# First layer norm: squares summed over the feature tiles by TensorE's accumulation instead of by VectorE's additions

## The chip, the cores and the metric

The kernel runs on one core of one Trainium2 chip. The metric is the device time of one execution in microseconds (us), the median of several runs. The engines named below are TensorE (PE in the rows; its weight loads are PEld), VectorE (DVE), ScalarE (ACT), GpSimd (POOL) and SyncE (SP), which issues most loads.

## The reference, cut to what matters

The program is one inference step of a hybrid decoder layer on 1024 prompt tokens and 32 sample tokens, 1056 in all, with 1024 features each, in float32. Its two branches (latent attention and a state-space scan) are merged and projected, and then two layer norms stand around a feed-forward network:

```
h = layer_norm(ALPHA * x + mix, ln1_g, ln1_b)
y = layer_norm(ALPHA * h + swiglu_ffn(h, ...), ln2_g, ln2_b)

def layer_norm(x, g, b, eps=1e-5):
    mu  = mean(x, axis=-1)
    var = mean(square(x - mu), axis=-1)
    return (x - mu) * rsqrt(var + eps) * g + b
```

The change concerns `var` of the first norm, that is, of `h`.

## The kernel before, in words

**Layout.** Activations are held with the features on the 128 partitions: `mm` is 128 x 8 x 1056, that is, KT = 8 feature tiles by all tokens. A sum over the features is therefore a sum over 8 tiles and over 128 partitions. The tokens are cut in three thirds of CH = 352 tokens, and a third in four blocks of TS = 88.

**The products.** Each float32 product with weights is written as three products of rounded halves (high by high, high by low, low by high: `whi`, `wlo`, `ahi`, `alo`). One output tile of one third is then 24 matrix products of 352 columns. `dense` makes a whole output tile (72 products), `unit_third(u, c)` that of one third c (24 products). GpSimd splits each weight tile into `whi` and `wlo` (`split`, L780 and L782) when TensorE has finished with the two tiles before.

**The stage in question.** There is no planner. Each engine has an order that is written out by hand, and engines wait for one another with semaphores. Around the first norm TensorE's order (L1594 to L1614) puts the last two output tiles of the projection (6 and 7) and the first two of the feed-forward (0 and 1) third by third, with the norm's small products between them: tiles 6 and 7 of third 0, tile 6 of third 1, `mean(0)`, tile 7 of third 1, tile 6 of third 2, `mean(1)`, `square_sums(0)`, tile 7 of third 2, `spread(0)`, `mean(2)`, `square_sums(1)`, feed-forward tile 0 of third 0, `spread(1)`, tile 1 of third 0, `square_sums(2)`, tile 0 of third 1, `spread(2)`, and the remaining three.

For a third c the norm goes as follows.

- VectorE adds the last two residual tiles and the running sum `srow` (`last_residual`, L2729 and L2734).
- TensorE multiplies `srow` by a matrix of ones (`mean`, L1576), ScalarE copies the result to `murow` (L2042), and VectorE subtracts it from all eight tiles (`centre`, L2741).
- ScalarE squares the eight tiles into `sqb` (128 x 8 x 352, `squares`, two activations, L2049; the traces call this memory `yz`). Before it writes `sqb` again it waits until the products of the third before are done (`sums_done`), and in its order `root_of(c)` of that third stands ahead of the next `squares`.
- VectorE adds the eight tiles to one in three halving steps (`add_squares`, L2748), and counts `squares_added`.
- TensorE sums tile 0 over the partitions: in `square_sums` (L1583) each of the four blocks of 88 tokens is loaded as weights and multiplied by one column of ones, so that one number for each token lands in a column of bank 7. A float32 product like this is two weight loads and two matrix products in the trace: four blocks are `x8`.
- ScalarE takes the root (`root_of`, L2054), VectorE the reciprocal (`inverse`, L2753), TensorE spreads it over the partitions (`spread`, L1591), and ScalarE copies it to `rsrow` (`factor_row`, L2059).
- VectorE scales the eight tiles (L2756), ScalarE adds the bias and rounds to `ahi` (L2064), and VectorE makes `alo` (L2767), all in `split_third`. The feed-forward products of this third wait tile by tile for `alo` (`g_split`).

VectorE's order is `last_residual(0)`, `centre(0)`, `last_residual(1)`, `add_squares()`, `centre(1)`, `inverse(0)`, `last_residual(2)`, `add_squares()`, `split_third(0)`, `centre(2)`, `inverse(1)`, `add_squares()`, `split_third(1)`, `inverse(2)`, `split_third(2)`. The sum of squares of the second norm and of the group norm is made elsewhere and is not touched.

Of the kernel before, what the change touches and what calls it, by code (L numbers as in the profile page):

```python
# [11 lines left out]
ALU = mybir.AluOpType  # L12
# [7 lines left out]
CH = TOK // 3  # L20
# [10 lines left out]
KT = D_MODEL // P  # L31
# [66 lines left out]
TS = 88  # L98
# [49 lines left out]
def build(nc, a, o, stop=99, debug=None):  # L148
# [23 lines left out]
    def sem(name):  # L172
        if name in taken:
            return sem(taken[name][0])
        if name not in sems:
            sems[name] = nc.alloc_semaphore(name)
        return sems[name]
# [52 lines left out]
    def const(name):  # L230
        at, n = where[name]
        return cst[:, at:at + n]

    ident, ones = const("ident"), const("ones")
    V_GATE, V_QN, V_KVN, V_SSM, V_L1G, V_L1B, V_L2G, V_L2B, V_END = 0, 16, 19, 21, 37, 45, 53, 61, 69

    ps = nc.alloc_psum_tensor("ps", [P, 8, 512], F32)
# [160 lines left out]
    mrow, nrow, nshift, nmax, total, ri_ = (ar(n, [P, 1]) for n in ("mrow", "nrow", "nshift", "nmax", "total", "ri_"))  # L398
# [58 lines left out]
    sqb = yz[:, :, :].rearrange("p a n -> p (a n)")[:, 0:KT * CH].rearrange("p (e n) -> p e n", n=CH)  # L457
# [310 lines left out]
    def _(pool):  # L768
# [71 lines left out]
        def ssm_scale(g, c):  # L840
            _, b, l, n = step_of(g, c)
            pool.wait_ge(sem("xd_ready"), k["xd_ready"].next())
            pool.tensor_tensor(s_xe[b][0:n], s_xd[b][0:n], dte[0:n, c, g * HG:(g + 1) * HG].unsqueeze(2).broadcast_to([n, HG, SP_]),
                               ALU.mult).then_inc(sem("xe_ready"), k["xe_ready"].adds(1))
# [64 lines left out]
    def _(pe):  # L909
        k = Counts()  # L910
# [178 lines left out]
        for v in range(2):  # L1089
            for j in range(NCONV // 2):  # L1090
                n = CW + 1 + NB * (CW - 1)
                last = pe.transpose(ps[:, 6 + v, j * n:(j + 1) * n], st[:, (v * 12 + j) * P:(v * 12 + j + 1) * P],
                                    ident[0:n, 0:n])
# [9 lines left out]
        for i in range(9):  # L1103
            n = P if i < 8 else NS
            last = pe.transpose(ps[0:n, 6, i * SH:(i + 1) * SH], dtr[:, i * P:i * P + n], ident[0:SH, 0:SH])
# [7 lines left out]
        last = pe.matmul(ps[0:NS, 6, 256:288], const("same_s")[0:NS], da[0:NS, 8], start=True, stop=True)  # L1113
# [3 lines left out]
        for i in range(8):  # L1117
            last = pe.matmul(ps[0:SH, 7 - i // 4, i % 4 * P:(i % 4 + 1) * P], da[:, i, :], const("causal"), start=True, stop=True)
# [3 lines left out]
        last = pe.matmul(ps[0:SH, 7, 0:NS], da[0:NS, 8, :], const("causal_s")[0:NS], start=True, stop=True)  # L1122
# [4 lines left out]
        for j in range(DI // P):  # L1127
            last = pe.matmul(ps[:, 6, j * NS:(j + 1) * NS], spread[0:SH, j * P:(j + 1) * P], act_[:, SEQ:TOK],
                             start=True, stop=True)
# [9 lines left out]
        def third():  # L1139

            t = thirds_done[0]
            u, c = divmod(t, 3)
            b, free = bank_of(t)
            thirds_done[0] += 1
            if c == 0:
                pe.wait_ge(sem("unit_split"), k["unit_split"].next())
            if t >= LEAD - 1:
                pe.wait_ge(sem(free), k[free].next())
            elif t == 0:
                pe.wait_ge(sem("out_free0"), k["out_free0"].next())  # L1150
            for i in range(3 * KT):
                j, part = divmod(i, 3)
                w, x = ((whi, xhi), (whi, xlo), (wlo, xhi))[part]
                last = pe.matmul(ps[:, b, 0:CH], w[u % SPLIT][:, j * P:(j + 1) * P], x[:, j, c * CH:(c + 1) * CH],  # L1154
                                 start=i == 0, stop=i == 3 * KT - 1)
            done = "unit_done" if c == 2 else "third_done"
            last.then_inc(sem(done), k[done].adds(1))
# [222 lines left out]
        for j in range(2):  # L1380
            for h in range(HEADS):
                last = pe.matmul(ps[:, j, h * NS:(h + 1) * NS], ukt[:, h, j * P:(j + 1) * P], qs[:, h, :], start=True, stop=True)
# [99 lines left out]
        for q in range(NB):  # L1482
            for j in range(2):
                last = pe.matmul(ps[:, 2 + j, q * HT:(q + 1) * HT], oseq[:, q, j * P:(j + 1) * P], const("fold")[:, 0:HT], start=True, stop=True)
        last.then_inc(sem("end_turned"), k["end_turned"].adds(1))
        pe.wait_ge(sem("end_read"), k["end_read"].next(2))
        for h in range(HEADS):
            r = 64 * (h % 2)
            for j in range(2):
                last = pe.matmul(ps[r:r + 64, 7, h // 2 * NS:(h // 2 + 1) * NS], wkv[:, j, h * P + NOPE:(h + 1) * P], olat[:, j, h, :],  # L1490
                                 start=j == 0, stop=j == 1)
# [66 lines left out]
        def unit_third(u, c, ready=None):  # L1558

            s = u % SPLIT  # L1560
            if c == 0:
                pe.wait_ge(sem("unit_split"), k["unit_split"].next())
                pe.wait_ge(sem(f"res_free{s}"), k[f"res_free{s}"].next())
            for i in range(3 * KT):
                j, part = divmod(i, 3)
                if ready and part == 0:
                    pe.wait_ge(sem(ready), k[ready].next())
                w, x = ((whi, ahi), (whi, alo), (wlo, ahi))[part]
                last = pe.matmul(ps[:, 3 * s + c, 0:CH], w[s][:, j * P:(j + 1) * P], x[:, j, third(c)], start=i == 0, stop=i == 3 * KT - 1)
            last.then_inc(sem("unit_done" if c == 2 else "third_ok"), k["unit_done" if c == 2 else "third_ok"].adds(1))  # L1570
# [7 lines left out]
        def square_sums(c):  # L1578

            pe.wait_ge(sem("row_read"), k["row_read"].held())  # L1580
            pe.wait_ge(sem("squares_added"), k["squares_added"].next())
            for t in range(CH // TS):
                last = pe.matmul(ps[0:TS, 7, CH + t:CH + t + 1], sqb[:, 0, t * TS:(t + 1) * TS], ones[:, 0:1], start=True, stop=True)  # L1583
            last.then_inc(sem("sums_done"), k["sums_done"].adds(1))

        def spread(c):
# [4 lines left out]
                last = pe.matmul(ps[:, 7, t * TS:(t + 1) * TS], inv[0:TS, at:at + 1].broadcast_to([TS, P]), ident[0:TS, 0:TS], start=True, stop=True)  # L1591
            last.then_inc(sem("row_ready"), k["row_ready"].adds(1))

        unit_third(6, 0)  # L1594
        unit_third(7, 0)
        unit_third(6, 1)
# [2 lines left out]
        unit_third(6, 2)  # L1599
        mean(1)  # L1600
        square_sums(0)
        unit_third(7, 2)
        spread(0)
# [504 lines left out]
    def _(dve):  # L2108
        k = Counts()
# [12 lines left out]
        step = k["dve_step"]  # L2122
# [26 lines left out]
        def add_squares(to, last):  # L2149
            name = "sq_ready" if last else "dve_step"  # L2150
            dve.tensor_tensor(sq[:, to], sq[:, to], sq[:, 1 - to], ALU.add).then_inc(sem(name), k[name].adds(1))
            if not last:
                dve.wait_ge(step.sem, step.same())
# [568 lines left out]
        def last_residual(c):  # L2722

            for b in range(2):
                if c == 0:
                    dve.wait_ge(sem(f"gt_full{b}"), k[f"gt_full{b}"].next(16))
                dve.wait_ge(sem("unit_done" if c == 2 else "third_ok"), k["unit_done" if c == 2 else "third_ok"].next())
                done = k[f"res_free{b}"] if c == 2 else step
                dve.scalar_tensor_tensor(out=mm[:, 6 + b, third(c)], in0=gt[b][:, third(c)], scalar=ALPHA,  # L2729
                                         in1=ps[:, 3 * b + c, 0:CH], op0=ALU.mult, op1=ALU.add).then_inc(done.sem, done.adds(1))  # L2730
                dve.wait_ge(done.sem, done.same())
                dve.wait_ge(step.sem, step.same())
                total = k["srow_ready"] if b else step
                dve.tensor_tensor(srow[:, third(c)], srow[:, third(c)], mm[:, 6 + b, third(c)], ALU.add).then_inc(total.sem, total.adds(1))  # L2734

        def centre(c):
            dve.wait_ge(sem("mu_ready"), k["mu_ready"].next())
            dve.wait_ge(sem("srow_ready"), k["srow_ready"].same())
            for h in range(2):
                part = mm[:, 4 * h:4 * h + 4, third(c)]  # L2740
                dve.tensor_tensor(part, part, murow[:, third(c)].unsqueeze(1).broadcast_to([P, 4, CH]), ALU.subtract).then_inc(sem("centred"), k["centred"].adds(1))  # L2741

        def add_squares():

            for h in (4, 2, 1):
                dve.wait_ge(sem("squared") if h == 4 else step.sem, k["squared"].next(2) if h == 4 else step.same())
                total = k["squares_added"] if h == 1 else step
                dve.tensor_tensor(sqb[:, 0:h, :], sqb[:, 0:h, :], sqb[:, h:2 * h, :], ALU.add).then_inc(total.sem, total.adds(1))  # L2748

        def inverse(c):  # L2750
            n = CH // TS
            dve.wait_ge(sem("rooted"), k["rooted"].next())
            dve.reciprocal(inv[0:TS, c * n:(c + 1) * n], stat[0:TS, c * n:(c + 1) * n]).then_inc(sem("inverted"), k["inverted"].adds(1))  # L2753
# [16 lines left out]
        last_residual(0)  # L2770
        centre(0)
        last_residual(1)
        add_squares()
        centre(1)
        inverse(0)
        last_residual(2)
        add_squares()
        for b in range(2):
            dve.nop().then_inc(sem(f"gt_free{b}"), k[f"gt_free{b}"].adds(1))
        split_third(0)  # L2780
        centre(2)
        inverse(1)
        add_squares()
        split_third(1)
        inverse(2)
        split_third(2)
# [90 lines left out]
```

## Time and profile before

| | us |
|---|---|
| median of 3 runs | 2907.76 (2906.79 to 2908.07) |
| the profiled execution, its own time | 2900.22 |
| its span, first to last instruction | 2898.4 |
| TensorE busy | 2824.4 (97%) |
| VectorE busy | 1478.2 (51%) |
| ScalarE busy | 736.7 (25%) |
| GpSimd busy | 1015.7 (35%) |
| mean granted clock of TensorE over the span | 0.98 of full |

The profile is of one execution. Its times count from the first instruction. The stage of the first norm lies between about 2048.7 us (tile 6 of third 0) and 2128.5 us (the first ordinary feed-forward tile), under 3% of the span. After it come some 720 us of feed-forward, nearly all of them TensorE products back to back.

### The profile page before, as it was taken

The page shows a single profiled execution, that of the slowest core. Times are in us where ns is not written, and L with a number is a line of the kernel's source. Part 1 is how long each engine was busy: PE and PEld are TensorE (multiplying, and loading weights), DVE is VectorE, ACT ScalarE, POOL GpSimd, SP SyncE. Part 2 cuts the span into 40 slices and gives each one's busy share as a digit, 9 for nine tenths or more (in the row PEclk, how much of TensorE's full clock was granted, in tenths as well). Part 3 has the DMA queues.
Part 4 walks back from the last instruction along what each step waited for, and adds up shares of the span by engine and source line. Part 5 has one row for each costly group of instructions (what it writes and reads, how often), then busy time and mean ns, then how long its engine had stood idle before and what let it go on. Part 6 is the DMA issues. An engine that isn't in the chain of part 4 may idle for free.

```text
span 2898.4 us, 45631 instructions
## 1 busy us (share of the span) xinstructions
PE 2824.4 (97%) x18894; PEld 2532.0 (87%) x18894; DVE 1478.2 (51%) x2052; ACT 736.7 (25%) x1154; POOL 1015.7 (35%) x603
## 2 busy tenths in 40 slices
PE   8999999999999999999999899999899999999998
PEld 7999999899999985555666699999799999999998
DVE  3535787765666665555444448765652222222226
ACT  2111212353545444454423222010220000000000
POOL 3443333333333323444211124344233333333331
PEclk9999999999999998999999999999899999999999
DMA  4263223564656545222343424353211111111111
GB/s 144 72 199 113 81 89 117 172 182 141 178 155 170 159 119 147 65 61 73 142 173 153 156 91 141 117 180 106 65 37 44 44 46 48 43 43 43 51 51 60
DMA packets 314769, 309.72 MB, mean 107 GB/s; under 512 B 32101, under 2 KB 273002, under 8 KB 312138
## 3 DMA queue, kind: packets, MB, share of 16 engines
q1 hardware_dynamic: 252392, 196.02, 23.8%
q10 hardware_dynamic: 58650, 73.89, 7.5%
q0 software_dynamic: 3584, 37.75, 3.4%
q8 instruction: 108, 1.77, 0.3%
q14 instruction: 35, 0.29, 0.0%
HBM read 229.41 MB, written 78.20 MB: 106 GB/s over the span
## 4 chain that ended last, share of the span: by engine, by line
PE 80%; DVE 12%; ACT 3%; issue 3%; DMA 1%; POOL 1%; ACTq 0%; SPq 0%; DVEq 0%; POOLq 0%
PE ps L973 42%; PE ps L1154 12%; PE ps L1288 4%; DVE cv L2252 3%; PE ps L1312 3%; PE ps L1302 2%; PE ps L1446 2%; PE ps L1402 2%; PE ps L1422 1%; PE ps L1187 1%; PE ps L1191 1%; PE ps L1180 1%; DVE cv L2246 1%; DVE cv L2254 1%; PE ps L937 1%
## 5 line engine op out<-in xcount | busy, mean ns | idle before, releaser
L780 POOL TENSOR_TENSOR whi<-raw,cst 128x1024 fp32r<-128x1024 f32 x160 | 311.9, 1949 | 1144.6 <-PE ps L973 937.4
L782 POOL TENSOR_TENSOR wlo<-raw,whi 128x1024 fp32r<-128x1024 f32 x160 | 433.1, 2707 | 12.6
L973 PE MATMUL ps<-ahi,whi 128*128 128x352 f32 x1728 | 375.7, 325 | 2.1 <-POOL wlo L782 1.4
L973 PE MATMUL ps<-alo,whi 128*128 128x352 f32 x1728 | 375.8, 326 | 0.0
L973 PE MATMUL ps<-ahi,wlo 128*128 128x352 f32 x1728 | 372.2, 324 | 0.0
L973 PEld LDWEIGHTS ps<-ahi,whi 128*128 128x128 f32 x1728 | 294.7, 189 | 2.7 <-POOL wlo L782 1.7
L973 PEld LDWEIGHTS ps<-ahi,wlo 128*128 128x128 f32 x1728 | 296.8, 189 | 0.0
L973 PEld LDWEIGHTS ps<-alo,whi 128*128 128x128 f32 x1728 | 295.6, 188 | 0.0
L1154 PE MATMUL ps<-xhi,whi 128*128 128x352 f32 x768 | 255.9, 333 | 0.4 <-ACT xraw L1764 0.4
L1154 PE MATMUL ps<-xhi,wlo 128*128 128x352 f32 x768 | 247.8, 323 | 0.0
L1154 PE MATMUL ps<-xlo,whi 128*128 128x352 f32 x768 | 247.7, 323 | 0.0
L886 POOL TENSOR_TENSOR pr<-pr,rowinv 128x384 f32<-128x384 f32 (+7 forms) x128 | 145.6, 1146 | 191.0 <-DVE rowinv L2458 190.7
L2453 DVE TENSOR_REDUCE negmax<-ps 128x1 f32<-128x384 f32 (+7 forms) x128 | 97.0, 758 | 139.1 <-PE ps L1290 138.4
L1288 PE MATMUL ps<-kb,qb 96*128 96x512 f32 (+3 forms) x384 | 160.2, 535 | 6.5 <-ACT pr L1892 3.3
L2640 DVE TENSOR_TENSOR mm<-ps,mm 128x1056 f32<-128x1056 f32 x80 | 100.6, 1258 | 116.3 <-PE ps L973 116.3
L973 PE MATMUL ps<-xhi,whi 128*128 128x352 f32 x672 | 148.0, 329 | 5.2 <-ACT xraw L1764 3.9
L1288 PEld LDWEIGHTS ps<-kb,qb 96*128 96x128 f32 x384 | 65.0, 196 | 100.4 <-issue 83.1
L1154 PEld LDWEIGHTS ps<-xhi,whi 128*128 128x128 f32 x768 | 144.3, 188 | 8.6 <-issue 6.2
L973 PE MATMUL ps<-xlo,whi 128*128 128x352 f32 x672 | 147.8, 329 | 0.0
L973 PE MATMUL ps<-xhi,wlo 128*128 128x352 f32 x672 | 146.2, 326 | 0.0
L1154 PEld LDWEIGHTS ps<-xlo,whi 128*128 128x128 f32 x768 | 144.4, 188 | 0.0
L1154 PEld LDWEIGHTS ps<-xhi,wlo 128*128 128x128 f32 x768 | 144.3, 188 | 0.0
(368 smaller groups left out, 5031.9 us busy)
## 6 DMA issues: line engine op xcount, KB each, us to landing
raw<-in_w_in SPq DMA_DIRECT2D x61, 512.0 KB, 5.0
s_a<-d_acum SPq DMA_DIRECT2D x32, 512.0 KB, 7.3
d_xbc<-so ACTq DMA_DIRECT2D x24, 528.0 KB, 2.7
gt<-d_g SPq DMA_DIRECT2D x24, 528.0 KB, 3.6
raw<-in_w_ffn_gate SPq DMA_DIRECT2D x22, 512.0 KB, 3.8
raw<-in_w_ffn_up SPq DMA_DIRECT2D x22, 512.0 KB, 3.8
raw<-in_w_ffn_down SPq DMA_DIRECT2D x22, 512.0 KB, 3.5
d_z<-zo ACTq DMA_DIRECT2D x16, 528.0 KB, 5.1
```

The source lines that it names most:

```text
L780: pool.tensor_tensor(whi[s][:, :], raw[:, u], ones[:, 0:1].broadcast_to([P, UNIT]), ALU.mult).then_inc(sem("unit_hi"), k["unit_hi"].adds(1))
L782: pool.tensor_tensor(wlo[s][:, :], raw[:, u], whi[s][:, :].bitcast(F32), ALU.subtract).then_inc(sem("unit_split"), k["unit_split"].adds(1))
L886: pool.tensor_tensor(pr[G][i][:, :], pr[G][i][:, :], rowinv[:, n:n + 1].broadcast_to([P, length]), ALU.mult).then_inc(sem("n_ready"), k["n ...
L973: last = pe.matmul(ps[0:m, 3 * b + c, 0:width], w(j), x[:, j, at:at + width], start=i == 0, stop=i == n - 1)
L1154: last = pe.matmul(ps[:, b, 0:CH], w[u % SPLIT][:, j * P:(j + 1) * P], x[:, j, c * CH:(c + 1) * CH], start=i == 0, stop=i == 3 * KT - 1)
L1288: pe.matmul(ps[:, first_bank + c // 512, 0:w], qb[pp][h][:, q * P:(q + 1) * P], kb[pp][h][:, c:c + w], start=True, stop=True)
L1302: last = pe.transpose(ps[:, 4 + h, c * P:(c + 1) * P], pr[G][2 * (3 - c) + h][:, kb_ * P:(kb_ + 1) * P], ident)
L1312: last = pe.matmul(ps[64 * h:64 * h + 64, 6 + G, c0 * P:512], vb[pp][h][:, kb_, :], ptb[kb_ % 2][h][:, c0 * P:512], start=first, stop=kb_ ...
L1402: last = pe.transpose(ps[:, 4 + i % 3, r * P:(r + 1) * P], src, ident)
L2252: dve.scalar_tensor_tensor(out=cv[b][:, 0:SEQ], in0=xraw[b][:, j:j + SEQ], scalar=tap(j), in1=cv[b][:, 0:SEQ], op0=ALU.mult, op1=ALU.add). ...
L2453: dve.tensor_reduce(negmax[:, n:n + 1], src, AX, ALU.max, negate=True).then_inc(sem("m_ready"), k["m_ready"].adds(1))
L2640: dve.tensor_tensor(thirds(mm[:, e]), out3(b), thirds(mm[:, e]), ALU.add).then_inc(sem(f"res_free{b}"), k[f"res_free{b}"].adds(1))
```

## The change

`square_sums` now multiplies all eight tiles of `sqb`, each block of 88 tokens accumulating over the eight tiles in its column of PSUM: 32 products for a third in place of 4. It waits for ScalarE's two `squared` counts in place of VectorE's `squares_added`. `add_squares` and its three calls go from VectorE's order. Nothing else is moved: the orders of all engines are the same otherwise. The line `k["squared"].n += 16` only sets where TensorE's count of that semaphore begins.

```diff
         def square_sums(c):
 
             pe.wait_ge(sem("row_read"), k["row_read"].held())
-            pe.wait_ge(sem("squares_added"), k["squares_added"].next())
+            pe.wait_ge(sem("squared"), k["squared"].next(2))
             for t in range(CH // TS):
-                last = pe.matmul(ps[0:TS, 7, CH + t:CH + t + 1], sqb[:, 0, t * TS:(t + 1) * TS], ones[:, 0:1], start=True, stop=True)
+                for e in range(KT):
+                    last = pe.matmul(ps[0:TS, 7, CH + t:CH + t + 1], sqb[:, e, t * TS:(t + 1) * TS], ones[:, 0:1], start=e == 0, stop=e == KT - 1)
             last.then_inc(sem("sums_done"), k["sums_done"].adds(1))
...
+        k["squared"].n += 16
         unit_third(6, 0)
...
-        def add_squares():
-
-            for h in (4, 2, 1):
-                dve.wait_ge(sem("squared") if h == 4 else step.sem, k["squared"].next(2) if h == 4 else step.same())
-                total = k["squares_added"] if h == 1 else step
-                dve.tensor_tensor(sqb[:, 0:h, :], sqb[:, 0:h, :], sqb[:, h:2 * h, :], ALU.add).then_inc(total.sem, total.adds(1))
-
...
         last_residual(0)
         centre(0)
         last_residual(1)
-        add_squares()
         centre(1)
         inverse(0)
         last_residual(2)
-        add_squares()
         for b in range(2):
             dve.nop().then_inc(sem(f"gt_free{b}"), k[f"gt_free{b}"].adds(1))
         split_third(0)
         centre(2)
         inverse(1)
-        add_squares()
         split_third(1)
```

## Rows read from the trace of the kernel before

**Rows 1.** The page: span, and each engine's busy time, share and instructions.
```profile
span 2898.4 us, 45631 instructions
PE 2824.4 (97%) x18894; PEld 2532.0 (87%) x18894; DVE 1478.2 (51%) x2052; ACT 736.7 (25%) x1154; POOL 1015.7 (35%) x603
```
**Rows 2.** Stretches: length, busy us of each engine (instructions), granted clock, DMA share, GB/s.
```profile
2071.20:2089.00 17.80, 9.29 (x50) 8.55 (x50) 17.33 (x15) 5.50 (x8) 8.64 (x4) 0.77 0.20 59
2089.00:2104.50 15.50, 12.92 (x45) 11.16 (x46) 13.75 (x22) 7.57 (x12) 0.00 (x0) 0.61 0.00 1
2104.50:2123.50 19.00, 17.72 (x103) 15.17 (x103) 16.36 (x33) 10.67 (x19) 0.07 (x1) 1.00 0.00 0
```
**Rows 3.** Chain that ended last, norm stage: start us, length us, engine, tile, line.
```profile
2054.33 7.97 PE ps L1569 x48
...
2071.21 2.11 DVE yz L2748
...
2073.45 0.85 PE ps L1583 x8
2074.31 5.43 PE ps L1569 x24
...
2082.08 3.69 DVE yz L2748
...
2087.16 0.59 DVE mm L2756
...
2113.45 0.48 ACT rsrow L2059
```
**Rows 4.** Timeline, TensorE: start, length, line, operation, count [idle before, releaser].
```profile
2070.42 0.75 PE L1576 MATMUL ps<-srow,cst 128*128 128x352 f32 x2
2074.61 0.49 PE L1569 MATMUL ps<-alo,whi 128*128 128x352 f32 x1
2074.90 0.49 PE L1569 MATMUL ps<-ahi,wlo 128*128 128x352 f32 x1
...
2087.39 1.31 PE L1583 MATMUL ps<-cst,yz 128*88 128x1 f32 x8 [4.40 <-DVE yz L2748]
...
2098.89 2.01 PE L1591 MATMUL ps<-cst,inv 88*128 88x88 f32 x8 [2.40 <-DVE inv L2753]
...
2106.39 0.71 PE L1583 MATMUL ps<-cst,yz 128*88 128x1 f32 x8
2106.97 0.41 PE L1569 MATMUL ps<-ahi,whi 128*128 128x352 f32 x1
```
**Rows 5.** Timeline, VectorE, the same columns.
```profile
2068.63 4.68 DVE L2748 TENSOR_TENSOR yz<-yz 128x1408 f32<-128x1408 f32 x3
...
2080.32 1.76 DVE L2734 TENSOR_TENSOR srow<-srow,mm 128x352 f32<-128x352 f32 x1
2082.00 5.25 DVE L2748 TENSOR_TENSOR yz<-yz 128x1408 f32<-128x1408 f32 x3
...
2100.19 3.11 DVE L2748 TENSOR_TENSOR yz<-yz 128x1408 f32<-128x1408 f32 x3 [1.36 <-ACT yz L2049]
2103.22 1.08 DVE L2756 SCALAR_TENSOR_TENSOR mm<-mm,vecs,rsrow 128x352 f32<-128x352 f32 x2
```
**Rows 6.** Timeline, ScalarE, the second half of third 0's squares.
```profile
2066.62 1.38 ACT L2049 ACTIVATE yz<-mm 128x1408 f32<-128x1408 f32 x1 [0.15 <-DVE mm L2741]
```
**Rows 7.** Stretches around one-column products and granted clock (columns as in rows 2).
```profile
94.50:96.60 2.10, 2.04 (x25) 1.89 (x25) 0.16 (x1) 0.00 (x0) 2.02 (x4) 1.00 0.00 0
...
97.50:99.40 1.90, 1.90 (x9) 1.90 (x8) 0.00 (x0) 0.00 (x0) 0.00 (x0) 0.54 0.35 96
...
2073.45:2074.20 0.75, 0.75 (x9) 0.75 (x9) 0.75 (x1) 0.00 (x0) 0.75 (x1) 0.84 0.00 0
2074.20:2077.00 2.80, 2.80 (x11) 2.80 (x12) 2.80 (x2) 0.26 (x1) 1.33 (x1) 0.50 0.02 6
2077.00:2079.50 2.50, 2.50 (x16) 2.50 (x15) 2.46 (x5) 2.31 (x2) 0.00 (x0) 0.92 0.69 203
```
**Rows 8.** Timeline, TensorE, group norm (L1506: the same one-column products, 12 blocks).
```profile
1669.59 3.68 PE L1506 MATMUL ps<-cst,sq 128*88 128x1 f32 x24
1673.13 1.23 PE L973 MATMUL ps<-ahi,whi 128*128 128x352 f32 x3
```
**Rows 9.** Stretch with these products (columns as in rows 2).
```profile
1669.60:1673.30 3.70, 3.70 (x27) 3.70 (x26) 2.81 (x3) 3.59 (x4) 0.00 (x0) 0.50 0.00 0
```

## The prediction, made before the changed kernel was timed

> **What bounds the kernel now.** I read the page first: TensorE is busy for 2824.4 of 2898.4 us, VectorE for half of it [rows 1]. So over the whole span TensorE sets the time, and work taken from VectorE is worth something only where TensorE waits for it. That is read from the stage of the first norm alone, in stretches [rows 2]. From 2071.2 to 2089.0 TensorE is busy for 9.3 of 17.8 us and VectorE for 17.3; from 2089.0 to 2104.5 TensorE is busy for 12.9 of 15.5, but at a granted clock of 0.61; from 2104.5 on both are busy at full clock. Here VectorE is the bound and TensorE pays twice, in waits and in a low clock after them. The chain of waits says the same [rows 3]: it runs over the last addition of squares at 2071.21, the one-column products at 2073.45, tile 7 of third 2, the additions at 2082.08, and later VectorE's scaling and low parts. The timelines give the waits: the mean's products end at about 2071.2 and the one-column products of third 0 start at 2073.45, 2.3 us later [rows 3, 4]; those of third 1 start after an idle 4.40 us, ended by the additions [rows 4]; those of third 2 at 2106.39 wait for nothing [rows 4], since the additions were over at 2103.3 [rows 5].
>
> **What goes.** VectorE loses 4.68 + 5.25 + 3.11 = 13.0 us [rows 5], and TensorE its waits of 2.3 and 4.4 us. The squares of third 0 end at 2066.62 + 1.38 = 2068.0 [rows 6], before TensorE's `mean(1)` is done, so its new wait costs nothing there.
>
> **What comes.** Each third has 32 float32 one-column products in place of 4, in the trace's count 64 pairs of weight load and product in place of 8. A pair takes (2106.97 - 2106.39) / 8 = 0.073 us at full clock [rows 4] and (1673.13 - 1669.59) / 24 = 0.147 us at half clock [rows 8, 9]. 64 pairs are 4.7 us at the one and 9.4 us at the other; over three thirds the 168 added pairs are 12.3 to 24.7 us of TensorE time, more than the 6.7 us of waits that go, even at the best clock. That they accumulate in one column I cost at nothing: the two pairs of one float32 product add to one column already.
>
> **Which clock.** In the stretch 94.5 to 96.6 TensorE ran 24 such pairs without a wait to speak of, busy for 2.04 of 2.10 us, and the clock was near half right behind them, 0.54 [rows 7]. From 1669.6 to 1673.3 it was busy all the time, nearly all of it in 24 such pairs, and stayed at 0.50 [rows 9]. After the 2.3 us of idle and 8 pairs from 2073.45 it fell (0.84, then 0.50), and came back within 2077.0 to 2079.5, after some 11 dense products at 0.29 us each in place of 0.166 [rows 3, 4, 7]. So a run of 64 pairs does not hold the clock as dense products do, and the dense unit behind it pays too: 5.43 us for 24 products where full clock needs 3.9 (7.97 / 2) and half clock 7.0 [rows 3, 4]. I take the clock to fall 2.8 us after dense work ends, as at 2071.2 to 2074.0: 38 pairs at 0.073 and 26 at 0.147 are 6.6 us. Where dense work stands right in front, as in third 2, I take 6.0; behind the wait for the last residual, as in third 1, 8.2.
>
> The Trainium skill (TensorE: Matmul & The Clock Gate, "What's actually happening") says that activity releases the throttle and that the clock follows how busy the engine has been. Taken by the busy share, back-to-back pairs would hold the clock at full and even close the waits that make it fall now. By that reading the time comes out as in the second case below, by my reading of rows 7 and 9 as here; the trace speaks against the busy share as the measure, for the engine was busy at 0.97 and 1.00 in those stretches.
>
> **The sum, along TensorE's order.** `square_sums(0)` starts at 2071.2 and takes 6.6: 2077.8, where it ended at 2074.3. Tile 7 of third 2 takes 5.4 as before: 2083.2, against 2079.7. VectorE's last residual and its addition take 2.3 us as before (the addition 1.76, held up beside GpSimd's split, which moves with it) [rows 5]: 2085.5. `mean(2)` 0.7: 2086.2. `square_sums(1)` 8.2: 2094.4, where it ended at 2088.7. ScalarE's squares of third 1 now wait for the root of third 0, at 2078.2, and need 3 us: done by 2081.3, hidden. Meanwhile VectorE starts `split_third(0)` at 2085.5 in place of 2087.16 [rows 3], and has nearly all eight tiles ready at 2094.4. Feed-forward tile 0 runs unhindered, 5.4: 2099.8. VectorE's `centre(2)` and `inverse(1)` are done by then. `spread(1)` and its copy take 1.5: 2101.3, which is where the copy ended before. `split_third(1)` then starts at 2101.3, 1.9 us ahead of 2103.22 [rows 5], because the third addition is gone. That gain is not used, since TensorE is late now: tile 1 of third 0 ends at 2104.4, `square_sums(2)` takes 6.0: 2110.4; tile 0 of third 1, partly at half clock, 5.8: 2116.2; `spread(2)` and the copy 1.5: 2117.7. Before, that copy ended at 2113.45 + 0.48 = 2113.93 [rows 3]. All that follows, the third split that paces the products and 720 us of dense work, is shifted as it is: 3.8 us later.
>
> Where the clock falls within a run varies from one execution to the next. If it falls early, the unit behind stands at 7.0 in place of 5.4. I add 0.7 us for that: +4.5 us. The profiled execution would go from 2900.2 to 2904.7 and its span from 2898.4 to about 2902.9. The median of the runs lies 7.5 us above the profiled one, outside anything this stage does, so I add the 4.5 to it: 2907.8 + 4.5 = 2912.3 us, 0.15% more.
>
> **The cases.**
>
> 1. As above, the pairs at mixed clock: +2 to +8 us, 2912.3. For it: rows 7 and 9. Chance 0.64. A measurement of this kernel can tell about 0.2%, 5.8 us, from no change; a fifth of this case lies above that.
>
> 2. The other side: the clock holds, since TensorE no longer idles in this stage. Then 4.7 us a run and 3.9 a unit: 2071.2 + 4.7 + 3.9 = 2079.8, last residual 2082.1, mean 2082.8, second run 2087.5, tile 0 paced by VectorE's split, which begins at about 2082.3 and ends at 2091.2, `centre(2)` 3.2, inverse, spread and copy 1.8: 2096.2 in place of 2101.4. Then 2095.9 + 3.9 + 4.7 + 3.9 = 2108.4, spread and copy: 2109.4, that is, 4.5 us earlier: 2903.3. It decides from the point at which the clock stays at full through `square_sums(1)` and `(2)`. Against it is the fall at 97.5. Chance 0.11.
>
> 3. The pairs run at half clock throughout or cost 0.1 us or more each even at full clock, and the units behind them stand at 7.0. Against 6.6, 8.2 and 6.0 a run of 9.4 adds 7.4 us, and up to 3 us come from the units, against slack of 0 to 2 us in the split: +8 to +14, 2918.8 in the middle. For it: the clock was at 0.61 from 2089.0 to 2104.5 already [rows 2], so little is needed to keep it down. Chance 0.2.
>
> The remaining 0.05 is for what I don't see, 0.03 of it on the faster side beyond 0.2%. The range is 2905.5 to 2918.5: it leaves out most of case 2 and half of case 3. Slower by over 0.2%: a fifth of case 1 and all of case 3, 0.33. Within 0.2%: the rest of case 1 and nearly all of case 2, 0.62. Faster 0.05: that 0.03, and 0.02 of case 2, whose 4.5 us are not far from 5.8.
>
> **What would show it.** In the changed profile the one-column products come as x64 three times; the first starts at about 2071.2 with no wait, and the second waits for the last residual's mean and not for squares. Each run takes 5.5 to 9 us, and the granted clock falls to half inside it or within 2 us behind. VectorE's busy time is down by 11 to 13 us, TensorE's up by 14 to 22. The copy to `rsrow` of third 2 ends near 2117.7; near 2109 would be case 2, past 2122 case 3. I am wrong if a run takes 4.7 us with dense units of 3.9 behind it, or if the pairs stretch beyond 0.147 us.

## The result, and the profile after

The changed kernel takes 2916.28 us (median of 8 runs) against 2909.48 for the kernel before (8 runs, the three shown above among them). The ratio is 1.0031, with a 95% interval of 1.0021 to 1.0041: 0.31% slower, about 9 us (the two medians differ by 6.8 us). One of the eight runs of the kernel before took 3933.37 us and is left out of the ratio. The forecast was 0.15%, with 2905.5 to 2918.5 as its range. The direction and the range held. The size is twice the forecast, and about half of it has a cause that the prediction did not name.

The page and the chain of waits of the changed kernel (start us, length us, engine, tile, line; x64 are the one-column products):

```profile
span 2911.9 us, 45958 instructions
PE 2839.5 (98%) x19062; PEld 2546.3 (87%) x19062; DVE 1471.5 (51%) x2043; ACT 736.7 (25%) x1154; POOL 1012.2 (35%) x603
```
```profile
2059.17 7.96 PE ps L1569 x48
...
2076.01 6.42 PE ps L1584 x64
2082.42 5.63 PE ps L1569 x24
...
2091.31 7.85 PE ps L1584 x64
2099.16 5.77 PE ps L1569 x24
2104.92 0.86 PE ps L1592 x8
2105.78 3.88 PE ps L1569 x24
2109.67 6.00 PE ps L1584 x64
2115.67 6.02 PE ps L1569 x24
...
2122.58 0.47 ACT rsrow L2061
...
2137.68 163.00 PE ps L973 x1008
2300.68 1.07 issue
2301.75 139.76 PE ps L973 x864
2441.51 0.67 issue
2442.18 139.75 PE ps L973 x864
2581.93 1.08 issue
2583.01 139.78 PE ps L973 x864
2722.80 0.62 issue
```

Set beside [rows 3], the chain has changed hands: where it ran through VectorE's additions, it now stays on TensorE from 2059.17 to 2122.56 but for the last residual of third 2. The first piece shown starts 4.84 us later than in the kernel before (2059.17 against 2054.33). That much comes from the part of the program ahead of the stage, which is the same in both: over the seven profiled executions without instructions added at the start of the program, the stage's first product comes anywhere from 2048.7 to 2058.8 us. So only lengths are compared below, not times.

The stretches name the two terms. First the kernel before, stage and feed-forward, then the changed one (columns as in rows 2):

```profile
2048.70:2128.50 79.80, 64.44 (x344) 58.02 (x342) 65.60 (x84) 27.85 (x41) 19.32 (x9) 0.87 0.11 34
2128.50:2849.50 721.00, 720.95 (x4464) 720.95 (x4465) 182.12 (x128) 47.34 (x44) 266.60 (x124) 1.00 0.15 45
```
```profile
2053.60:2137.70 84.10, 78.72 (x512) 75.83 (x511) 56.12 (x75) 27.71 (x41) 20.11 (x9) 0.86 0.11 32
2137.70:2863.00 725.30, 721.86 (x4464) 720.71 (x4465) 182.13 (x128) 47.34 (x44) 266.96 (x124) 1.00 0.15 46
```

The norm's stage grew from 79.8 to 84.1 us, 4.3 more. The feed-forward, in which nothing is changed, grew from 721.0 to 725.3, another 4.3. Its products are the same 4464, and the loss stands in the chain above: a gap of 0.6 to 1.1 us, put down to "issue", at each of the four places where TensorE's loop jumps back, 3.4 us in all; the chain does not resolve the rest. In the kernel before, this whole stretch has no gap:

```profile
2128.55 720.48 PE ps L973 x4460
```

The queue that carries instructions shows what goes on there (kind, packets, MB, share), first before, then after:

```profile
q8 instruction: 8, 0.13, 0.1%
```
```profile
q8 instruction: 44, 0.72, 0.4%
```

4.3 + 4.3 = 8.6 us are 0.30%, close to the measured 0.31%. These are two single executions, and the stage varies from one to the next (below), so that the sum agrees to 0.01% is partly luck.

### The profile page after: what moved, and what is told of

Its sections match the earlier page's. It is cut to its first block, busy times and chain, and to the rows that moved or that the text cites. A ratio compares the mean times of both kernels' runs of the same rounds, so it can differ in the third digit from the quotient of the medians.

```text
span 2911.9 us, 45958 instructions
## 1 busy us (share of the span) xinstructions
PE 2839.5 (98%) x19062; PEld 2546.3 (87%) x19062; DVE 1471.5 (51%) x2043; ACT 736.7 (25%) x1154; POOL 1012.2 (35%) x603
## 4 chain that ended last, share of the span: by engine, by line
PE 81%; DVE 11%; ACT 3%; issue 2%; DMA 1%; POOL 1%; ACTq 0%; SPq 0%; DVEq 0%; POOLq 0%
PE ps L973 42%; PE ps L1154 12%; PE ps L1288 4%; DVE cv L2254 3%; PE ps L1312 2%; PE ps L1302 2%; PE ps L1422 2%; PE ps L1446 2%; PE ps L1402 2%; PE ps L1569 1%; DVE cv L2248 1%; PE ps L1187 1%; PE ps L1191 1%; PE ps L1180 1%; PE ps L1067 1%
```

## The experiments

Ten kernels were run. All stretches below run from the stage's first product to the first ordinary feed-forward tile ("stage"), and from there to the first product of the last tiles ("feed-forward"). Each ratio is against the kernel before on the same chip. Every kernel was profiled once, so the length of a stage is that of one execution.

**Two theories of the second term.** The program of TensorE has 336 more instructions in front of the loop: 84 products, each in four instructions (two weight loads and two matrix products). Counted in the assembled program, the loop is 1764 instructions long, at 64 bytes 6.9 fetches of 16 KB (0.72 MB in 44). It begins 236 instructions behind a multiple of 256 in the kernel before and 60 behind one in the changed kernel.

The first experiment moves the loop alone, by 80 instructions:

```diff
 (kernel before, start of TensorE's program)
+        for _ in range(160):
+            pe.wait_ge(sem('eps_ready'), 1)
```
(Two such waits on a count that stands already make one instruction.)

> The kernel before, with 80 instructions added at the very start of TensorE's program (each waits for two semaphore counts that stand already), where TensorE idles until 8.5 us for its input. All work is the same; the loop of the feed-forward stands 80 instructions later in the program, which is where the changed kernel has it but for whole multiples of 256 (it has 336 more). Theory A (the 4.4 us that the changed kernel loses after the norm come from fetching TensorE's instructions again at each turn of the loop, because of where the loop stands): the norm stage stays as before, gaps of 0.6 to 1.1 us stand at each of the four jumps back, instruction fetches there go from 8 to about 44, and the kernel is 3 to 5 us slower (0.10 to 0.17%). Theory B (the loss comes from the norm stage, a clock or a buffer that is late): no gaps, 8 fetches, and the same time within 1.5 us.

Measured: ratio 1.0014 (1.0003 to 1.0025), 4.1 us; the medians differ by 2.5. The stage is 81.2 us, the feed-forward 725.1, the fetches are 44, and the gaps are there:

```profile
2142.92 163.04 PE ps L975 x1008
2305.96 1.07 issue
2307.04 139.75 PE ps L975 x864
2446.78 0.78 issue
...
2587.34 0.63 issue
...
2727.72 0.65 issue
```

Theory A holds: with all work as before, the feed-forward is 4.1 us longer, and only the place of the loop differs there. (The padding is not quite free: the first product comes at 9.71 us in place of 8.47, so up to 1.2 us of the timed difference may be the padding's.) The second moves the changed kernel's loop by 176 further, to a whole 512 (`range(352)` at the same place).

> The changed kernel, with 176 such waiting instructions at the start of TensorE's program, so that with the 336 of the products the loop of the feed-forward is moved by 512 in all, twice 256. Theory A: the gaps at the jumps back are gone, the norm stage keeps its loss of 3.5 to 5 us against before, and the kernel is 4 to 5 us slower than before in place of some 9 (0.14 to 0.17%). Theory B: still gaps, still about 0.3% slower.

Measured: 8 fetches, no gap, the feed-forward 720.9, the stage 82.6. But the ratio is 1.0064 (1.0050 to 1.0079). The mechanism is as theory A said; the expected time was missed, because the padding is not free where I put it: the first product comes at 20.0 us in place of 8.5. These 11.6 us and some 3 to 4 us of stage make up the 15.5 us by which the medians differ. The fix puts the same 176 behind every second product of the projection's last dense tiles, inside `products`:

```diff
+                    if fill[0] and (3 * i + c) % 2:
+                        fill[0] -= 1
+                        for _ in range(2):
+                            pe.wait_ge(sem('eps_ready'), 1)
...
+        fill[0] = 176
         for u in range(6):
             dense(u, u % 2, ahi, alo, KT, ...)
```

> The changed kernel with the same 176 added waiting instructions as e2, but one behind every second product of the dense tiles of the last projection, where TensorE's sequencer has time, in place of the start of the program (there the first transpose came at 20.0 us in place of 8.4). The loop of the feed-forward stands where it stood in e2. If the loss of the changed kernel is two terms, norm stage and loop, this kernel has only the first: 7 to 8 instruction fetches in the loop, no gaps, feed-forward 721 us, stage 82 to 85 us against 79.8 before, 3 to 5 us slower than before (0.10 to 0.17%). If the place of the loop were not the cause of its gaps but the padding at the start, the gaps come back and it is 0.3% slower. If the padding isn't hidden here, the last projection takes longer by up to 20 us.

Measured: 1.0020 (1.0005 to 1.0035), 8 fetches, the feed-forward 720.9, the stage 87.3. So the padding is hidden, the loop term is gone, and the stage term stands alone. The stage is longer than in the other runs of the same arrangement (84.1, 82.6) and than the 82 to 85 expected. The clock accounts for most of that: with the same products, the three runs of 64 pairs take 7.20, 9.45 and 6.60 us here and 5.10, 8.06 and 6.22 in e2, 3.9 us more, and the granted clock in them is 0.68, 0.50 and 0.75 against 1.00, 0.60 and 0.80.

Where may the loop stand? Two kernels, each executed once:

> The kernel before with 20 waiting instructions at the start of TensorE's program. The loop of the feed-forward is 1764 TensorE instructions long in the program; before, it began 236 instructions behind a multiple of 256, here it begins at 256, in e1 it began 60 behind. Fetches in the traces move 16 KB, 256 instructions of 64 bytes. Theory A1 (the loop is kept as long as it lies in 7 such blocks, which a length of 1764 allows at 29 of 256 places; where blocks begin on the chip is not known): at most one of this kernel and the next can be free of gaps, since they stand 46 apart. Theory A2 (a wider range of places is good, 8 blocks too): both are free of gaps, 8 fetches each and 721 us.

> The changed kernel with 150 waiting instructions at the start of TensorE's program: its loop begins 210 instructions behind a multiple of 256, 26 before the place of the kernel before. Theory A1: gaps here or in the kernel with 20, or in both, with some 44 fetches and 725 us for the feed-forward. Theory A2: none in either. The norm stage is that of the changed kernel, 82 to 88 us.

Measured: 20 further on, 17 fetches and one gap of 2.7 us, feed-forward 723.9. 26 before: 44 fetches and 744.9 us, 24 us lost, with two gaps at each jump, one of them behind a single product, 13.5 us in all, and turns of 141 to 142 us in place of 139.8. The turns are longer because of the clock: behind the first pair of gaps it is 0.62 and 0.51 of full until 2314 us, behind the second 0.50 until 2458. The chain:

```profile
2143.51 163.04 PE ps L975 x1008
2306.55 0.73 issue
2307.29 0.42 PE ps L975
2307.71 2.38 issue
2310.09 141.14 PE ps L975 x863
```

Theory A2 falls: neither place is free. A1 asked only that at most one be free, and it doesn't explain why, 20 further on, the loop turns three times without a gap and fetches again at one jump alone. A double gap would fit a loop whose head lies in the last few instructions of a fetched block; no run shows that, nor where blocks begin. What is shown is that the place decides; which rule it follows stays open. The Trainium skill (Runtime: NRT & Kernel Launch, "Instruction fetch mechanics") states 16 KiB blocks, and that a taken branch whose target is not in the current window of two pages stalls until the page is fetched. The packets (0.72 MB in 44) and the gaps of the changed kernel agree. By a window of two pages each jump back over 6.9 blocks would have to fetch and stall; the kernel before speaks against that, with 8 fetches in five turns and no gap. That section of the Trainium skill also gives TensorE's store as 128 KiB, which would hold a loop of 6.9 blocks.

**The two halves of the change, apart.** First the removal. This kernel leaves seven of the eight feature tiles out of the sum of squares; it shows only what the time would be.

```diff
 (changed kernel)
-                for e in range(KT):
-                    last = pe.matmul(..., sqb[:, e, ...], ones[:, 0:1], start=e == 0, stop=e == KT - 1)
+                last = pe.matmul(..., sqb[:, 0, ...], ones[:, 0:1], start=True, stop=True)
```

> The removal alone: VectorE's additions are left out and TensorE still makes only the 4 products of feature tile 0 for each third, so the variance is that of one tile of eight (part of the sum is left out). The program of TensorE has the length of before. Theory 1 (the additions did cost the waits and the removal is worth what the stage then gives): no wait of TensorE for squares, the copy to rsrow of third 2 comes 4 to 9 us earlier against the start of the stage, and the kernel is 4 to 9 us faster (0.15 to 0.3%). Rival: ScalarE's squares and VectorE's scaling are the bound anyway, and under 2 us come of it.

Measured: ratio 0.9980 (0.9968 to 0.9993). Stage 73.9, feed-forward 721.0. The removal is worth 5.9 us of stage, within theory 1's 4 to 9; TensorE's waits for squares are gone, and what it still waits for is VectorE's residual, its reciprocals and low parts. Then the products:

```diff
 (kernel before)
-                last = pe.matmul(ps[0:TS, 7, CH + t:CH + t + 1], sqb[:, 0, ...], ones[:, 0:1], start=True, stop=True)
+                for e in (1, 2, 3, 4, 5, 6, 7, 0):
+                    to = CH + t if e == 0 else CH + 4 + t
+                    last = pe.matmul(ps[0:TS, 7, to:to + 1], sqb[:, e, ...], ones[:, 0:1], start=e < 2, stop=e in (0, 7))
```

> The products alone: VectorE's additions stay, and TensorE makes 28 more one-column products for each third, of the feature tiles 1 to 7 into spare columns that nobody reads; padding as in f1. If the two parts of the change simply add up, and the removal is worth 5.9 us of stage (e3: 73.9 against 79.8), the products cost the difference to the changed kernel's 82.6 to 84.1, so the stage here is 88 to 91 us and the kernel 9 to 11 us slower than before. If instead the products hide where TensorE has to wait for the additions anyway, under 86 us.

Measured: ratio 1.0056 (1.0037 to 1.0075), stage 93.5, feed-forward 721.0. The products cost 13.6 us of stage, more than the 8 to 11 expected. Its runs of 64 pairs:

```profile
2078.56 7.15 PE L1592 MATMUL ps<-cst,yz 128*88 128x1 f32 x64 [2.28 <-DVE yz L2757]
...
2100.03 9.52 PE L1592 MATMUL ps<-cst,yz 128*88 128x1 f32 x64 [3.83 <-DVE yz L2757]
...
2120.80 5.21 PE L1592 MATMUL ps<-cst,yz 128*88 128x1 f32 x64
```

Behind an idle wait of 3.83 us the run takes 9.52 us, as long as 64 pairs take at half clock (9.4); behind dense work 5.21. Removal and products sum to 13.6 - 5.9 = 7.7, the two together cost 2.6 to 7.4 (stages of 82.5 to 87.3 against a mean of 79.9), so by single executions the sum can't be told from the two together. Whether the waits for the additions make the products dearer, by a lower clock, is not shown: f1 has no such wait and its second run takes 9.45 us.

**Is it the clock, and does it stay up with more columns?** Same weight loads, same pairs, but 80 columns of ones in place of one:

```diff
 (changed kernel, padded as e2)
-                    last = pe.matmul(ps[0:TS, 7, CH + t:CH + t + 1], sqb[:, e, ...], ones[:, 0:1], ...)
+                    last = pe.matmul(ps[0:TS, 7, CH + t:CH + t + 80], sqb[:, e, ...], ones[:, 0:80], ...)
```

> The changed kernel with 176 instructions of padding as in e2, and each product multiplied by 80 columns of ones in place of 1 (the columns behind the wanted one are overwritten by the next block or not read). The weight loads, which set the pace at full clock, are the same. Theory 1 (one-column products don't hold the clock, what counts is columns streamed): the clock stays at full through the three runs and the units behind them, 64 pairs take 4.7 to 5.5 us in place of 6 to 8 and the units 3.9 to 4.5 in place of 5.4 to 6.0, the stage is 5 to 10 us shorter than in e2, and the kernel 1 to 5 us faster than before. Theory 2 (the clock follows how busy the engine is, or falls for the waits of the stage alone): same clock and same time as e2. If float32 products of 80 columns are slower than the weight load, the runs take over 5.5 us even at full clock.

Measured: the stage is 78.9 us where e2 has 82.6, and the ratio 1.0038 (1.0024 to 1.0052), with the padding's delay at the start in it. Both fall short of what theory 1 was to bring (a stage 5 to 10 us shorter, a kernel faster than before), and the clock did not stay up through all three runs. The stretches of the changed kernel over its three runs and the units behind them, and under them the first of each with 80 columns:

```profile
2075.80:2082.40 6.60, 6.60 (x66) 6.55 (x64) 5.86 (x2) 0.46 (x1) 5.19 (x2) 0.75 0.00 1
2082.40:2088.00 5.60, 5.60 (x27) 5.60 (x27) 1.26 (x4) 2.79 (x3) 0.00 (x0) 0.68 0.32 92
2091.20:2099.20 8.00, 8.00 (x66) 8.00 (x65) 7.84 (x14) 4.38 (x8) 1.40 (x1) 0.60 0.23 68
2099.20:2105.00 5.80, 5.80 (x27) 5.80 (x28) 4.71 (x6) 3.21 (x5) 0.00 (x0) 0.67 0.00 0
2109.70:2115.70 6.00, 6.00 (x64) 6.00 (x64) 4.98 (x10) 2.91 (x5) 0.00 (x0) 0.80 0.00 0
2115.70:2121.70 6.00, 6.00 (x26) 6.00 (x27) 0.17 (x1) 0.26 (x1) 0.00 (x0) 0.63 0.00 0
```
```profile
2084.90:2090.10 5.20, 5.20 (x66) 5.20 (x65) 4.50 (x2) 0.46 (x1) 5.12 (x2) 1.00 0.00 0
2090.10:2094.00 3.90, 3.90 (x27) 3.90 (x26) 2.55 (x5) 2.92 (x3) 0.04 (x1) 1.00 0.46 134
```

In the changed kernel TensorE is busy in every one of the six stretches from end to end, and its clock is 0.60 to 0.80 of full. With 80 columns it holds 1.00 through the first run and its unit. Of the three runs only the one that starts behind the residual's wait still falls (6.50 us; the others 5.17), and once more where TensorE waits 2.3 us for a reciprocal. At full clock the float32 product of 80 columns costs next to nothing over one of a single column: 5.17 us for 64 pairs, against 5.10 in e2, where the clock stood at 1.00 through the first run of one-column products too and at 0.69 in the unit behind.

What then bounds the stage is VectorE again. The chain of e4 leaves TensorE behind tile 7 of third 2 and comes back to it 16 us later (f4 has the same pieces, 2083.30 to 2099.36):

```profile
2090.07 3.90 PE ps L1571 x24
...
2093.99 0.53 DVE mm L2733
...
2096.24 2.68 DVE mm L2753
...
2106.76 3.15 DVE mm L2745 x2
2109.91 0.09 DVE inv L2750
...
2110.05 1.70 PE ps L1594 x8
2111.75 4.88 PE ps L1571 x24
2116.64 5.00 PE ps L1586 x64
```

The second run of pairs, 6.50 us, is not on this chain: its low clock costs nothing.

The same with the hidden padding, on the chip of f1:

> All 8 tiles on TensorE with 80 columns of ones, as e4, with the padding hidden as in f1. Stage 78 to 80 us, feed-forward 721 us: the same time as before within 2 us, or up to 1 us faster (0 to 0.05%), and 3 to 4 us faster than f1, which differs from it by the columns of the products alone. If the clock had nothing to do with the columns, f1 and f4 would have the same stage.

Measured: ratio 1.0000 (0.9990 to 1.0011), stage 78.8, feed-forward 721.0. Its median is 2905.57 us against f1's 2913.80 and 2905.73 for the kernel before. The two differ in the width of the products alone, and the stages differ by 8.5 us. Both differences are about twice the 3 to 4 us expected, since f1's stage came out long; against the mean of the changed arrangement, 84.1 us, the wider products shorten the stage by 5.3.

**A division of the work.** VectorE's first halving stays (`for h in (4,)`), TensorE accumulates four tiles with 80 columns, with 112 hidden padding instructions.

> A division of the work: VectorE makes the first halving of the additions (8 tiles to 4) and TensorE accumulates the remaining 4 tiles, 32 pairs for each third, each with 80 columns of ones as in e4; 112 added waiting instructions as in f1 so that the loop keeps its place. Theory 1 (TensorE's time is the bound in the changed kernel and the clock is lost to one-column products): a run takes 2.5 us, the clock falls only in VectorE's waits, and the stage is 75 to 78 us, between adds_gone (73.9) and wide (78.9): 2 to 5 us faster than before (0.07 to 0.17%). Rival: the halving stands behind the squares of the same third and in front of the next centring on VectorE, which gives back what TensorE saves; then 79 us or more and no gain.

Measured: stage 75.8, feed-forward 721.0; ratio 0.9997 (0.9985 to 1.0008), 2903.09 us against 2905.73. The three runs of 32 pairs take 2.66, 4.02 and 2.66 us. The stage is 4 us shorter than before, as expected, but the timed difference (2.6 us between medians) can't be told from none. It beats the changed kernel's arrangement in f1 (2903.09 against 2913.80 us); that it beats the kernel before is not shown.

## Why the prediction came out as it did, point by point

- **The waits that go, 2.3 and 4.4 us, and the bound passing to TensorE:** right. In the changed kernel no product waits for squares; what is left from 2059.17 to the third copy is the 1.55 us for the last residual.
- **The added pairs at mixed clock:** right as a mechanism. 6.6, 8.2 and 6.0 us were forecast for the three runs, 6.42, 7.85 and 6.00 stand in the chain; the units behind them 5.4, 5.4 and 5.8 against 5.63, 5.77 and 6.02. That it fits to 0.4 us is partly luck: over the four profiles of this arrangement the runs take 5.10 to 7.20, 7.74 to 9.45 and 5.88 to 6.60 us. The rows were also one-sided. Of the runs of 24 pairs in the kernel before, the prediction showed those with a low clock in or behind them; at 57.48 and 1759.77 us the same 24 pairs take 1.97 and 2.01 us, and the dense products behind them run at full clock. Whether the clock falls was less sure than rows 7 and 9 make it look.
- **The stage's sum:** right. The third copy to `rsrow` was to end 3.8 us later against the stage; it ends at 2123.05, which is 2118.21 less the stage's shift of 4.84, against 2113.93: 4.3. VectorE's busy time falls by 6.7 us over the span where 11 to 13 were forecast. In the stage it falls by 9.5 (65.60 to 56.12), less than the 13.0 of the additions' durations, since other operations grew: one scaling of `split_third(0)` takes 2.67 us in place of 0.58. It starts at 2090.32, while GpSimd splits a weight tile, and ends 0.4 us behind that split (2092.99 against 2092.60); the addition of 1.76 us in [rows 5] ran beside a split too. TensorE's busy time grew by 15.1 us, within the 14 to 22 forecast.
- **"All that follows ... is shifted as it is: 3.8 us later":** this is the step that failed, in its second half. The feed-forward was taken to be independent of the change because no operation in it was touched. It is 4.3 us longer, because 336 instructions were put in front of a loop that turned without a gap at its old place and fetches its instructions again at the new one: 44 fetches in place of 8 (shown by e1, e2 and f1; g1 and g2 show two other places). The gaps alone are 3.4 us. No case of the prediction had this term; with it, the sum would have been 4.5 + 4.3 = 8.8 us, 0.30%.
- **The spread between executions** that the prediction put at 0.7 us is larger: four profiles of the changed arrangement have stages of 84.1, 82.6, 87.3 and 82.5 us (mean 84.1), three of the old one 79.8, 78.8 and 81.2 (mean 79.9). The mean difference is 4.2.
- **The rival of a clock that holds** did not occur, but was reached by e4 and f4 with wider products, and gave less than its 4.5 us: 1.0 us of stage. From the end of `mean(1)` to the third copy e4 takes 41.8 us, where the rival had 38.2. Up to the end of `spread(1)`, 1.7 us of the difference lie on VectorE's part of the chain, where a scaling takes 2.68 us in place of 0.58; 1.0 in the unit behind the wait for the reciprocal, 4.88 us in place of 3.9; 0.6 in the pairs, 5.0 us on the chain in place of the 4.7 that I had from 8 pairs. The Trainium skill (TensorE: Matmul & The Clock Gate, "What's actually happening") lets the clock follow how busy TensorE has been. If busy is read as the share of time in which it works, that doesn't tell the first run of the changed kernel from that of e4: the share was 1 in both, and the clock 0.75 and 1.00.

## What to carry to other kernels

Before instructions are added ahead of a long hardware loop, see in the profile whether the loop turns without a gap and how many instruction fetches it makes; here an edit elsewhere that changed the count cost 4.3 us in a place that the edit never touches. Work that was moved to TensorE as one-column products was paid twice, in the pairs themselves and in the clock of the dense products behind them; with 80 moving columns the pairs took the same time at full clock, and the kernel was back at the time of before. An engine that is busy for 97% of the span is a poor place for more work: the waits that it could give here were 6.7 us, and the work put into them was at least 12.

## What the runs showed of the hardware that was not expected

- The place of a TensorE loop of 1764 instructions changes the time of the feed-forward that holds its five turns from 721 us to 724, 725 or 745, with 8, 17, 44 and 44 fetches (724 and 745 from one execution each).
- An instruction that waits for two counts which stand already takes about 0.11 us of TensorE's sequencer when many follow one another: with 80, 150 and 176 of them at the start (e1, g2, e2) the first product comes at 9.71, 17.27 and 20.03 us. Behind every second dense product 176 of them cost nothing that the profile shows.
- 64 pairs of weight load (88 columns) and float32 product take 5.1 to 5.2 us whether one column is streamed or 80, if the clock is full, and up to 9.5 us for one column otherwise.
- With one column, the granted clock over the three runs of 64 pairs and the units behind them is 0.50 to 1.00 (the changed kernel, e2 and f1), though TensorE is busy from end to end.
